# Norms around the dense feed-forward by pairs of token blocks, and the first expert's rows by a permutation product, in a two-layer transformer trunk

## The reference

```python
for l in range(2):
    h = modulate(rmsnorm(x, pre_mix_g[l]), shift, scale)       # latent and context rows
    p = h @ w_in[l]                                            # 1024 -> 2560
    o = concat(diff_attention(p), spatial_gating(p)) @ w_out[l]
    x = x + gate * rmsnorm(o, post_mix_g[l])
    f = modulate(rmsnorm(x, pre_ffn_g[l]), shift2, scale2)
    if l == 0:   # dense, width 2816
        y = (silu(f @ w1) * (f @ w3)) @ w2
    else:        # top 2 of 8 experts, width 3584, latent rows only
        y = sum over the chosen e of g[e] * (silu(f @ w1[e]) * (f @ w3[e])) @ w2[e]
    x = x + gate2 * rmsnorm(y, post_ffn_g[l])
```

## Time and profile before

| | |
|---|---|
| runs (us) | 1857.22, 1858.80, 1866.17; median 1858.8 |
| profiled execution | 1856.84 us, span of the trace 1855.0 us |
| granted TensorE clock, mean | 0.972 |
| PE, DVE, ACT, POOL busy | 1721.8, 1415.9, 1104.2, 71.0 us |
| DMA | 505.78 MB, mean 273 GB/s |

### The profile page before, as it was taken

How to read it: one execution, slowest core, us unless ns; L and a number is a source line. 1 busy time by engine, 2 the same in 40 slices (tenths; PEclk the granted TensorE clock), 3 DMA queues, 4 the chain that set the end, 5 groups by cost and what they waited for, 6 DMA issues and landing times.

```text
span 1855.0 us, 24268 instructions
## 1 busy us (share of the span) xinstructions
PE 1721.8 (93%) x8008; PEld 1394.6 (75%) x8008; DVE 1415.9 (76%) x1647; ACT 1104.2 (60%) x1415; POOL 71.0 (4%) x91
## 2 busy tenths in 40 slices
PE   6999889999999969975999999999999999999993
PEld 3766677888778757664888888888888888888882
DVE  3847757475664486763999999999999999999994
ACT  3345544222222253544888888888888888888883
POOL 0112200000010000300000000000000000000000
PEclk9999999999999989996999999999999999999997
DMA  9945316575574336243999999999999999999992
GB/s 324 253 128 190 138 46 205 168 226 179 185 250 158 121 106 234 80 149 129 373 377 367 393 369 381 388 358 395 376 367 393 355 396 380 365 392 359 388 377 87
DMA packets 229520, 505.78 MB, mean 273 GB/s; under 512 B 16377, under 2 KB 47249, under 8 KB 229185
## 3 DMA queue, kind: packets, MB, share of 16 engines
q1 hardware_dynamic: 225216, 493.30, 74.2%
q0 software_dynamic: 4224, 11.47, 2.3%
HBM read 497.34 MB, written 19.96 MB: 279 GB/s over the span
## 4 chain that ended last, share of the span: by engine, by line
issue 54%; PE 35%; DVE 6%; ACT 3%; DMA 2%; SPq 0%; POOL 0%; POOLq 0%; ACTq 0%; DVEq 0%
PE ps L600 10%; PE ps L602 10%; PE ps L601 10%; DVE w_lo L1380 1%; DMA raw<-in_ffn_w 1%; PE ps L797 1%; PE ps L833 1%; PE ps L669 1%; DVE xs L1559 1%; DMA raw<-in_ada_w 1%; DVE hT_lo L1532 1%; ACT w_hi L1072 1%; DVE att L1633 0%; PE ps L821 0%; PE ps L652 0%
## 5 line engine op out<-in xcount | busy, mean ns | idle before, releaser
L1380 DVE TENSOR_TENSOR w_lo<-raw,w_hi 128x1024 fp32r<-128x1024 f32 x570 | 684.9, 1222 | 209.8 <-ACT w_hi L1072 176.2
L1292 ACT ACTIVATE w_hi<-raw 128x1024 fp32r<-128x1024 f32 x448 | 473.9, 1062 | 105.6 <-PE ps L602 105.6
L600 PE MATMUL ps<-w_hi,he_hi 128*128 128x512 f32 x896 | 354.3, 395 | 0.7 <-DVE he_lo L1788 0.7
L602 PE MATMUL ps<-w_hi,he_lo 128*128 128x512 f32 x896 | 350.0, 391 | 0.0
L601 PE MATMUL ps<-w_lo,he_hi 128*128 128x512 f32 x896 | 349.3, 390 | 0.0
L1380 DVE TENSOR_TENSOR w_lo<-raw_more,w_hi 128x1024 fp32r<-128x1024 f32 x224 | 274.0, 1225 | 45.5 <-ACT w_hi L1292 25.5
L1292 ACT ACTIVATE w_hi<-raw_more 128x1024 fp32r<-128x1024 f32 x224 | 237.8, 1063 | 53.5 <-PE ps L602 53.5
L1072 ACT ACTIVATE w_hi<-raw 128x1024 fp32r<-128x1024 f32 x122 | 128.3, 1061 | 221.7 <-PE ps L602 197.5
L602 PEld LDWEIGHTS ps<-w_hi,he_lo 128*128 128x128 f32 x896 | 168.4, 188 | 35.9
L600 PEld LDWEIGHTS ps<-w_hi,he_hi 128*128 128x128 f32 x896 | 168.7, 188 | 34.8 <-issue 1.0
L601 PEld LDWEIGHTS ps<-w_lo,he_hi 128*128 128x128 f32 x896 | 168.8, 188 | 33.9
(11 more groups left out here) (231 smaller groups left out, 2003.4 us busy)
## 6 DMA issues: line engine op xcount, KB each, us to landing
raw<-in_moe_w SPq DMA_DIRECT2D x448, 512.0 KB, 6.0
raw_more<-in_moe_w SPq DMA_DIRECT2D x224, 512.0 KB, 6.1
raw<-in_ada_w SPq DMA_DIRECT2D x96, 512.0 KB, 4.6
raw<-in_ffn_w SPq DMA_DIRECT2D x66, 512.0 KB, 4.8
raw<-in_w_in SPq DMA_DIRECT2D x40, 512.0 KB, 6.4
raw<-in_w_out SPq DMA_DIRECT2D x16, 512.0 KB, 4.6
yrows<-in_x SPq DMA_DIRECT2D x8, 512.0 KB, 7.8
xe<-xrows SPq DMA_DIRECT2D x8, 512.0 KB, 6.4
```

Source lines behind the costliest of these rows:

```text
L600: pe.matmul(o, lh, rh, start=start, stop=False)
L602: return pe.matmul(o, ll, rh, start=False, stop=stop)
L1292: act.activation(w_hi[:, s % SPL, :], expert_raw(i), ACT.Copy).then_inc(hi_done, 1)
L1380: dve.tensor_tensor(w_lo[:, s_ % SPL, :], src, w_hi[:, s_ % SPL, :].bitcast(F32), ALU.subtract)\
```

## The change

Four things. (1) Layer 0's norm ahead of the feed-forward: `xn` of blocks 0 and 1 is transposed behind block 2's part of the output projection and ahead of block 3's, and modulated and split there (`turn_block`, `modulate_pair`, `split_pair`); the feed-forward's first matmuls wait per k for the second pair's split. (2) Behind the feed-forward the norm goes by pairs (`norm_after_ffn` on ACT and DVE), and `project_after_ffn` starts layer 1's first projection on blocks 0 and 1 while blocks 2 and 3 are normed; layer 1's eight `acc` units come four units later, and two groups of `mod_a` columns are made a little later. (3) Expert 0's rows in turn 0 are made on PE as `hrow` times a permutation `perm`, with no DRAM in between; SP's wait for the scatter moves from unit 16 to unit 40 of expert 0; two splits move behind the routing numbers; ACT loads its next function table early (a one-element Silu behind the Exp). (4) The tail: POOL itself waits for `y kept` and reads `flag`, each gather has its own semaphore, sums, gates, residuals and output transfers go by halves of 512 columns, and a one-element Sqrt stands ahead of them.

The diff, cut to its core:

```diff
-                acc(1 + l if 3 <= 4 * jn + u < 11 else 0)
+                acc(1 + l if (3, 7)[l] <= 4 * jn + u < (11, 15)[l] else 0)
...
-                        if first and i == (0 if turn else XIN_FIRST):
-                            if turn:
-                                take_x(0)
...
+                            if first and not turn:
                                 sp.wait_ge(sg("x sent"), 16 * 2 * NLAT)
-                                sp.dma_start(xe[:, :], xv[0][0]).then_inc(sg("xe in"), 16)
-                        if i == XIN_AT and not last:
...
-            sp.sem_inc(sg("y all"), 1)
             for b in range(NLAT):
-                sp.wait_ge(sg("final x"), b + 1)
-                sp.dma_start(out.rearrange("a (b p) d -> p (a b) d", p=P)[:, b, :], xs[:, b, :]).then_inc(s_out, 16)
-            sp.wait_ge(s_out, 16 * NLAT)
+                for half in range(2):
+                    o = slice(512 * half, 512 * half + 512)
+                    sp.wait_ge(sg("final x"), 2 * b + half + 1)
+                    sp.dma_start(out.rearrange("a (b p) d -> p (a b) d", p=P)[:, b, o], xs[:, b, o]).then_inc(s_out, 16)
+            sp.wait_ge(s_out, 32 * NLAT)
...
+            busiest = pool.value_load(flag[0:1, 0:1], min_val=0, max_val=NLAT * P)
+            pool.wait_ge(sg("y kept"), 16 * NE)
+            with pool.If(busiest > P):
+                pool.wait_ge(sg("y kept"), 32 * NE)
             for tb in range(NLAT):
...
-                        .then_inc(sg("y got%d" % tb), 16)
+                        .then_inc(sg("y got%d%d" % (tb, j)), 16)
...
+            def turn_block(key, b):
+                pe.wait_ge(sg("xn " + key), b + 1)
+                if key == "mix1" and b >= 2:
+                    pe.wait_ge(sg("hT32 mix1"), KD)
+                for k in range(KD):
+                    m = pe.transpose(pair_at(key, b // 2, k)[:, P * (b % 2):P * (b % 2) + P], xn[:, b, P * k:P * k + P], ident)
+                    if b % 2:
+                        m.then_inc(sg("hT ps " + key), 1)
+            def project_after_ffn():
+                def part(jn, u, i, blocks):
+                    h, lo = (view(t, u) for t in split_at(u.s))
+                    for kk in range(2):
+                        k = 2 * i + kk
+                        for b in blocks:
+                            if jn + b // 2 == 0 or (jn == 1 and b == 2):
+                                pe.wait_ge(sg("hT mix1"), k + 1 if jn == 0 else KD + max(k + 1, 4))
+                            m = mm3(ps[:, 4 * jn + b, :], hT_hi[:, k, P * b:P * b + P], hT_lo[:, k, P * b:P * b + P],
+                                    h[:, kk, :], lo[:, kk, :], k == 0, k == KD - 1)
+                    return m
+                turn_block("mix1", 0)
+                turn_block("mix1", 1)
+                pe.wait_ge(sg("mod fin"), len(MODS))
+                for i, u in enumerate(at["in", 1, IN_ORDER[0]]):
+                    pe.wait_ge(lo_done, u.s + 1)
+                    part(0, u, i, (0, 1)).then_inc(unit_used, 1)
+                us = at["in", 1, IN_ORDER[1]]
+                for i in range(2):
+                    turn_block("mix1", 2 + i)
+                    pe.wait_ge(lo_done, us[i].s + 1)
+                    part(1, us[i], i, (0, 1))
+                for i, u in enumerate(us):
+                    if i >= 2:
+                        pe.wait_ge(lo_done, u.s + 1)
+                    part(1, u, i, (2, 3) if i < 2 else range(NB)).then_inc(unit_used, 1)
...
+                    if l == 0 and b == 2:
+                        pe.wait_ge(sg("z pm0"), NB + 2)
+                        turn_block("ffn0", 0)
...
-                                if c + wi == 0:
-                                    pe.wait_ge(sg("hT ffn0"), 4 * i + 4)
...
+                                        if c + wi + ci == 0:
+                                            pe.wait_ge(sg("hT ffn0"), KD + k + 1)
...
+                pe.wait_ge(sg("route consts"), 1)
+                pe.matmul(ps[:, 2, P:2 * P], ones_r[:, :], triu_r[:, :], start=True, stop=True)
...
+            def gather_first():
+                pe.wait_ge(sg("hrow"), NLAT)
+                pe.wait_ge(sg("perm"), NLAT)
+                for k in range(KD):
+                    for tb in range(NLAT):
+                        m = pe.matmul(ps[:, 4 + k // 4, P * (k % 4):P * (k % 4) + P], hrow[:, tb, P * k:P * k + P], perm[:, tb, :],
+                                      start=(tb == 0), stop=(tb == NLAT - 1))
...
+                for k in ks:
+                    if k == 0:
+                        act.wait_ge(sg("ada fin"), len(ADA_SEQ))
+                        if l:
+                            act.wait_ge(sg("mod fin"), 2)
+                    act.wait_ge(sg("hT ps " + key), KD * p + (k | 1) + 1)
+                    act.activation(hT32(key)[:, k, 256 * p:256 * p + 256], pair_at(key, p, k), ACT.Identity,
+                                   bias=mod_b[:, l, which, k, p:p + 1], scale=mod_a[:, l, which, k, p:p + 1])\
+                        .then_inc(sg("hT32 " + key), 1)
...
+            def norm_after_ffn():
+                first = first_units["mix1"]
+                ffn_square(1, 0)
+                ffn_square(1, 1)
+                post_root_pair(0)
+                pre_square("mix1", 1, 0, 0)
+                ffn_square(1, 2)
+                pre_root("mix1", 0)
+                pre_square("mix1", 1, 0, 1)
+                ffn_square(1, 3)
+                pre_root("mix1", 1)
+                modulate_pair("mix1", 1, 0, 0, range(4))
+                post_root_pair(1)
+                split_upto(first + 3)
+                modulate_pair("mix1", 1, 0, 0, (4, 5))
+                pre_square("mix1", 1, 0, 2)
+                modulate_pair("mix1", 1, 0, 0, (6,))
+                pre_root("mix1", 2)
+                pre_square("mix1", 1, 0, 3)
+                modulate_pair("mix1", 1, 0, 0, (7,))
+                pre_root("mix1", 3)
+                split_upto(first + 5)
+                modulate_pair("mix1", 1, 0, 1, range(4))
+                split_upto(first + 6)
+                modulate_pair("mix1", 1, 0, 1, range(4, KD))
...
                     act.activation(st[:, 24 + b:25 + b], st[:, 20 + b:21 + b], ACT.Sqrt).then_inc(sg("rt pm%d" % l), 1)
+                    if l == 0 and b == 2:
+                        modulate_pair("ffn0", 0, 1, 0, range(4))
+                    if l == 0 and b == 3:
+                        split_upto(first_units["ffn0"])
                     pre_square("ffn%d" % l, l, 1, b)
                     pre_root("ffn%d" % l, b)
...
+                                    ffn_square(0, b)
+                    act.activation(st2[:, 127:128], cst[:, C_ONES:C_ONES + 1], ACT.Sqrt)
...
             act.activation(rs[:, 82:84], rs[:, 80:82], ACT.Exp).then_inc(sg("gap exp"), 1)
+            act.activation(st2[:, 127:128], cst[:, C_ONES:C_ONES + 1], ACT.Silu)
...
+            act.activation(st2[:, 127:128], cst[:, C_ONES:C_ONES + 1], ACT.Sqrt)
             act.wait_ge(sg("gates"), 1)
...
+            def split_pair(key, p, ks):
+                o = slice(256 * p, 256 * p + 256)
+                for k in ks:
+                    dve.wait_ge(sg("hT32 " + key), KD * p + k + 1)
+                    link(dve.tensor_copy(hT_hi[:, k, o], hT32(key)[:, k, o]))
+                    dve.tensor_tensor(hT_lo[:, k, o], hT32(key)[:, k, o], hT_hi[:, k, o].bitcast(F32), ALU.subtract)\
+                        .then_inc(sg("hT " + key), 1)
...
+            def norm_after_ffn():
+                first = first_units["mix1"]
+                update = residual(y0, "x ffn")
+                post_root_pair(0)
+                update(0)
+                update(1)
+                pre_mean("mix1", 0)
+                pre_scale("mix1", 0)
+                pre_mean("mix1", 1)
+                pre_scale("mix1", 1)
+                split_pair("mix1", 0, (0, 1))
+                ffn_gates(0, (2, 3))
+                split_pair("mix1", 0, (2,))
+                ffn_gates(1, (2, 3))
+                post_mean_pair(1)
+                split_pair("mix1", 0, (3,))
+                split_upto(first + 3)
+                post_root_pair(1)
+                update(2)
+                split_pair("mix1", 0, (4,))
+                update(3)
+                pre_mean("mix1", 2)
+                split_pair("mix1", 0, (5,))
+                pre_scale("mix1", 2)
+                pre_mean("mix1", 3)
+                split_pair("mix1", 0, (6,))
+                pre_scale("mix1", 3)
+                split_pair("mix1", 0, (7,))
+                split_upto(first + 5)
+                split_pair("mix1", 1, range(4))
+                split_upto(first + 6)
+                split_pair("mix1", 1, range(4, KD))
...
+                            if g == len(groups) - 1 and b == 1:
+                                ffn_gates(n2, (0, 1))
+                                if n2:
+                                    post_mean_pair(0)
...
+                rank0 = rs[:, 32:34]
```

(12 more changed lines are left out.)

236 lines of the change are left out of this document (149 added, 87 removed).

## The result

| | before | after |
|---|---|---|
| median of 5 runs (us) | 1857.22 (1856.1 to 1866.17) | 1826.77 (1824.48 to 1829.66) |
| span of the profiled execution | 1855.0 | 1825.0 |
| granted TensorE clock, mean | 0.972 | 0.980 |

A forecast was written before the change was run, and what follows sets the result against it. TensorE was taken to set the expert stage's pace, with gains only in its four gaps: 1 + 3 + 16 + 3.5 = 23.5 us, against the median 1858.8 giving 1835.3, say 1835; range 1826 to 1844.

The forecast's parts named there:

- Four later `acc` units ... may be late; I take 3: Ahead of attention: displaced VectorE work may be late, so of 4.1 us remaining after the second projection, 3 are taken.
- The bound: Expert stage: TensorE sets the pace; an earlier start is carried whole to the end, edits inside adding no matmuls gain nothing.
- Rival (c): Expert stage fed no faster than transfers come, so the router gain is given back: gain 7.5, time 1851; chance 0.04.
- rival (d): Granted clock falls in the expert stage after a shorter pause; at 0.97 the time is 1864; chance 0.02.
- Rival (a): Norms by pairs give nothing, VectorE's list being on the path: -1 and -1 for 1 and 3, time 1841; chance 0.13.
- Rival (b): More than forecast: products at fast clock 1.6, POOL's branch nothing 1.4, behind the feed-forward 4; time 1828; chance 0.09.
- Part 1: forecast 1: Ahead of the feed-forward: block 3's xn 4 us later, first matmul at 280.8; gain 1 us, bounds -1 and +3.
- Part 2: forecast 3: Behind the feed-forward: layer 1's first projection matmul 8.7 us earlier, 3 us kept; bounds 0 and 7.
- Part 3: forecast 16: Router: first expert matmul at 853.9 or 855.5 instead of 870.5; gain 16 us, lower bound 13, upper 17.5.
- The rule on table loads: Router, ACT: skill's 2.66 us per table switch would cost 2.8 us more, leaving 13 there and time near 1838.
- The row: Profile row of ACT's table load: 1.28 us and nothing besides, giving 16 us at the router.
- Part 4: forecast 3.5: Tail: POOL's own wait 2 us, halves and early table 1.3, output transfers 0.2; gain 3.5, bounds 1.5 and 5.5.

The follow-up runs named there:

- p3_only: Kernel before with the third part alone (permutation product, two splits behind the routing numbers, early Silu table); median 1840.42 us, ratio 0.9909 to before.
- norms_only: Kernel before with the first two parts alone (norms by pairs, later acc units); median 1849.05 us, ratio 0.9955 to before.
- acc_early: Changed kernel with layer 1's acc units back at places 3 to 10; median 1831.55 us, ratio 0.9857 to before.
- no_part1: Changed kernel with layer 0's transposes, modulations and splits of all four blocks behind the output projection again; median 1834.92 us, ratio 0.9885 to before.
- mod_early: Changed kernel, Exp and table loads behind he_hi, gate numbers behind he_lo, k=4,5 of blocks 0,1 modulated and split earlier; 1824.62 us, ratio 0.9818 to before.
- fill_long: Kernel before with 84 identity transposes on TensorE ahead of the wait for xe; median 1857.12 us, ratio 0.9995 to before.

## Why the forecast was too small

The mechanisms held; what failed is the size of terms. The step that missed most is the end of part 2, "Four later `acc` units ... may be late; I take 3", where 5.2 was measured. Next comes a term that part 3 left at nothing: the matmuls that run at the low clock behind the wait for `xe`, 1.5 us. Smaller misses are 1.0 us in part 1, 0.5 in part 3's chain and 0.6 in part 4.

**The bound.** Right: an earlier start of the expert stage is carried to the end (`p3_only`: span 16.1 less, median 18.5 less). Rival (c), that the DMA-fed stage gives it back, and rival (d), that the clock falls in it, are refuted; the stage got shorter, with granted clock 1.00 in its first 13.9 us (`p3_only`). Rival (a), no gain from the norms by pairs, is refuted by `norms_only` (interval below 1). Rival (b) named 1828, near the 1826.77 measured, but its terms did not come: the products took 5.34 us, and where they took 3.81 this gave 0.3 us and not 1.6 (`p3_only`, `acc_early`); POOL's wait gave 0.7 beyond the forecast and not 1.4, part 2 gave 2.2 and not 4. That its sum is near is mostly luck.

**Part 1: forecast 1, about 1.2 to its first matmul, and more behind.** The steps were right (block 3's `xn` 4.1 later, first matmul 280.93 for 280.8). First feed-forward matmul without part 1, six traces: 281.7 to 283.1, mean 282.4; with it, eight traces: 280.2 to 284.6, mean 281.2. What I didn't price: behind a wait of 6.01 ten matmuls followed each other at the low clock's 0.43 us, behind waits of 2.0 and 0.3 six, and four times 0.2 is 0.8 us. All traces bear this out. From the last output-projection matmul to the first of the feed-forward it is 13.3 us in the six and 10.2 in the eight; the 16 transposes that now stand earlier take about 2 of the 3.1 (eight take 1.09), so 1 is left, as forecast. Slow matmuls behind it: 7 to 14 in the six, 5 to 7 in the eight. The feed-forward's own length swings between 372.7 and 378.5, because in seven of the fourteen traces the granted clock falls once or twice within it, with part 1 and without: near 545 us behind a wait of 2.0 to 3.0 us, and between 645 and 650 behind one of 1.82 us that all fourteen have and behind which it falls in four. The same stretch of the kernel before and of `no_part1`:

```profile
545.00:549.00 4.00, 4.00 (x19) 3.29 (x19) 0.45 (x1) 0.51 (x1) 0.00 (x0) 1.00 1.11 363
545.00:549.00 4.00, 4.00 (x13) 3.10 (x12) 1.87 (x3) 0.00 (x0) 0.00 (x0) 0.57 1.10 350
```

Where it does not fall, the feed-forward takes 374.8 and 374.9 us without part 1 and 372.7 to 374.0 in the five traces with it: the 0.8 and a little more.

**Part 2: forecast 3, measured 5.2 (6.0 in the one pair of traces above).** From the last feed-forward matmul to the router's first, five traces without it: 178.9 to 179.9; the six with it and its `acc` order as in the change, `mod_early` left out: 176.7, 171.1, 173.6, 173.6, 173.5, 176.6 (and 170.9 with fillers). Their mean is 174.2 against 179.4, the gain 5.2 (2.7 to 8.3, by attention's clock). Up to the first turn of q and k the sets lie closer, 60.9 to 61.9 and 56.0 to 57.2 us, and the gain is 4.8 there already. Two steps failed. "Four later acc units ... may be late; I take 3" had the wrong sign: from q and k's first turn to attention's first scores it is 21.5 us in all fourteen traces, nothing is late there, and leaving the units where they were costs 2.5 (`acc_early`). The change also moves them in layer 1 alone, not "per layer". And the first matmul came 11.6 us behind the last of the feed-forward, where 12.8 was forecast: the root waits for two blocks, so the residual starts 3.4 us behind that matmul and not 4.0, and the transposes follow. That VectorE's list paces the first projection was right: 15.6 forecast, 16.1 measured (15.2 where the clock does not fall in it).

**Part 3: forecast 16, measured 16.5 and 1.5.** The chain came out as worked out, with products of 5.34 us between the two prices (3.9 and 7.7), which hardly mattered, as ACT's list ended beside them; both `perm` and `he_hi` were within 0.3 us of their place. The term that was missing is the expert stage's first matmuls at the low clock: I read clock 0.57 in the gap and used it for the products, but not for what stands behind the gap, 1.5 us (`fill_long`).

**The rule on table loads.** The row decided: two switches cost 2 x 1.28 us and no drain; the activation behind the second load starts 0.02 us after its end, `he_hi` 0.11 later. By the Trainium skill's 1.38 us of drain for each of the two ("ScalarE: Activation LUTs", "What ACT_TABLE_LOAD costs") it would have started near 847; the trace disagrees.

**Part 4: forecast 3.5, measured 4.1.** The terms were differently split: POOL's own wait brought 2.67 (2 forecast, inside 0.4 to 3.4), the gathers' own semaphores and half-rows 0.45 from the first gather to the second scale and 0.42 from there to the last residual (1.3 forecast), the halved output transfers 0.5.

**Sum.** 1.2 + 0.8 + 5.2 + 18.0 + 4.1 = 29.3 of 30.4 us. Of the 6.9 us beyond the forecast, 2.3 are clock behind shortened gaps (parts 1 and 3), 2.2 lie in part 2, 0.5 in part 3's chain, 0.6 in the tail and 0.2 in part 1's start. Of part 2's 2.2, 1.1 is the charge for the `acc` units, which was not due; what else part 2 brought is not taken apart. The last 1.1 of the 30.4 us lie within the spread of the clock between executions and aren't settled.
